# Two hybrid decoder layers on one core: the eight expert passes alternate between the 128-row and the 64-row form

## The reference, cut to what matters

```
def swiglu(h, w1, w3, w2):
    return (jax.nn.silu(h @ w1) * (h @ w3)) @ w2

def moe_swiglu(h, w_router, w1, w3, w2):
    logits = (h @ w_router).astype(jnp.float32)
    top_val, top_idx = lax.top_k(logits, TOP_K)          # TOP_K = 2
    top_w = jax.nn.softmax(top_val, axis=-1)
    combine = jnp.sum(jax.nn.one_hot(top_idx, N_EXPERTS) * top_w[..., None], axis=-2)
    out = jnp.zeros_like(h)
    for e in range(N_EXPERTS):                           # 8 experts, inner width 3584
        out = out + combine[..., e:e + 1] * swiglu(h, w1[e], w3[e], w2[e])
    return out
```

## Time and profile before

| | |
|---|---|
| median of three runs | 1884.23 us (1883.58 to 1884.46) |
| profiled execution, its own time | 1884.23 us |
| its span (first to last instruction) | 1882.5 us |
| PE busy | 1807.6 us, 96% |
| DVE busy | 1527.5 us, 81% |
| ACT busy | 1240.2 us, 66% |
| read from memory | 511.74 MB |

### The profile page before, as it was taken

How to read it: one execution, slowest core, us unless ns; L and a number is a source line. 1 busy time by engine, 2 the same in 40 slices (tenths; PEclk the granted TensorE clock), 3 DMA queues, 4 the chain that set the end, 5 groups by cost and what they waited for, 6 DMA issues and landing times.

```text
span 1882.5 us, 25226 instructions
## 1 busy us (share of the span) xinstructions
PE 1807.6 (96%) x10094; PEld 1534.7 (82%) x10094; DVE 1527.5 (81%) x1402; ACT 1240.2 (66%) x1144; POOL 73.8 (4%) x97
## 2 busy tenths in 40 slices
PE   9999999999999999999999999999998989888897
PEld 9989998999999998998878888888886656666665
DVE  7999965575568999764688888888889979889796
ACT  5656745454455565655667777777778878788785
POOL 1000000100010000000100000001000000000000
PEclk9999999999999999999999999999999999999998
DMA  8544544355545445553689999999999999999992
GB/s 331 179 176 154 183 162 183 140 188 180 197 166 181 179 138 196 204 182 132 226 319 402 377 379 362 406 370 364 401 363 390 421 350 419 382 372 416 353 418 109
DMA packets 75845, 519.91 MB, mean 276 GB/s; under 512 B 9360, under 2 KB 9616, under 8 KB 14544
## 3 DMA queue, kind: packets, MB, share of 16 engines
q1 hardware_dynamic: 72464, 507.84, 70.3%
q0 software_dynamic: 2544, 9.18, 1.7%
q10 hardware_dynamic: 720, 1.31, 0.2%
HBM read 511.74 MB, written 6.55 MB: 275 GB/s over the span
## 4 chain that ended last, share of the span: by engine, by line
PE 77%; DVE 10%; ACT 6%; issue 5%; DMA 1%; SPq 0%; ACTq 0%; DVEq 0%
PE psum L1903 15%; PE psum L1889 13%; PE psum L1891 13%; PE psum L1890 13%; PE psum L1904 7%; DVE wlo L1164 7%; ACT whi L629 5%; PE psum L2391 5%; PE psum L2392 4%; PE psum L2410 1%; PE psum L2404 1%; DVE U L1742 1%; PE psum L2157 1%; PE psum L2137 1%; DMA raw<-in_stream 1%
## 5 line engine op out<-in xcount | busy, mean ns | idle before, releaser
L1164 DVE TENSOR_TENSOR wlo<-raw,whi 128x2048 fp32r<-128x2048 f32 x369 | 839.0, 2281 | 214.9 <-ACT whi L629 214.3
L629 ACT ACTIVATE whi<-raw 128x2048 fp32r<-128x2048 f32 x369 | 699.3, 1902 | 150.3 <-PE psum L1891 76.9
L1903 PE MATMUL psum<-h_hl,whi 128*128 128x512 f32 x1216 | 430.3, 398 | 0.3 <-DVE U L1522 0.2
L1904 PE MATMUL psum<-h_hl,wlo 128*128 128x256 f32 x1216 | 340.1, 280 | 0.0
L2391 PE MATMUL psum<-whi,act_hl 128*128 128x512 f32 x672 | 286.6, 426 | 41.0 <-DVE wlo L1164 36.9
L1889 PE MATMUL psum<-whi,act_hl 128*128 128x512 f32 x736 | 291.3, 396 | 4.3 <-DVE wlo L1164 4.1
L1891 PE MATMUL psum<-whi,act_hl 128*128 128x512 f32 x736 | 287.5, 391 | 0.0
L1890 PE MATMUL psum<-wlo,act_hl 128*128 128x512 f32 x736 | 287.2, 390 | 0.0
L1903 PEld LDWEIGHTS psum<-h_hl,whi 128*128 128x128 f32 x1216 | 228.2, 188 | 55.3 <-issue 1.2
L2392 PE MATMUL psum<-wlo,act_hl 128*128 128x512 f32 x672 | 269.2, 401 | 0.0
L1904 PEld LDWEIGHTS psum<-h_hl,wlo 128*128 128x128 f32 x1216 | 229.5, 189 | 0.1
(11 more groups left out here) (291 smaller groups left out, 2076.3 us busy)
## 6 DMA issues: line engine op xcount, KB each, us to landing
raw<-in_stream SPq DMA_DIRECT2D x366, 1024.0 KB, 6.7
U<-in_stream SPq DMA_DIRECT2D x74, 1024.0 KB, 7.4
memhat<-in_stream SPq DMA_DIRECT2D x37, 1024.0 KB, 7.3
raw<-in_stream SPq DMA_DIRECT2D x6, 512.0 KB, 3.7
xacc<-U POOLq DMA_DIRECT2D x3, 512.0 KB, 7.6
xT<-in_x_cols ACTq DMA_DIRECT2D x4, 256.0 KB, 6.5
raw<-in_stream SPq DMA_DIRECT2D x4, 256.0 KB, 6.9
memhat<-in_mem_cols SPq DMA_DIRECT2D x1, 1024.0 KB, 20.0
```

The costliest lines, as they stand in the source:

```text
L629: act.activation(whi[:, n % SPLIT, 0:words], src[:, 0:words], ACT.Copy).then_inc(hi_ready, 1)
L1164: dve.tensor_tensor(wlo[:, n % SPLIT, 0:words], src[:, 0:words], whi[:, n % SPLIT, 0:words].bitcast(F32), ALU.subtract).then_inc(lo_ready, 1)
L1903: pe.matmul(o[:].rearrange("p (a b) -> p a b", a=2), st[0], mv, start=start, stop=False)
L1904: return pe.matmul(o[:, 0:256], st[1], mv[:, 0, :], start=False, stop=stop)
```

## The change

`few(p)` is true for the odd passes and no longer for p of 4 and above, so the order of forms is full, few, full, few, and so on. The tables follow: the ranks 1 to 4 go to passes 1, 3, 5, 7 and the ranks above to passes 2, 4, 6; `cap` and the slots of the experts likewise. `folded_rows` leaves the branch that only a few step has, because now a full pass comes after a few pass and has to fold its result.

```
 def few(p):
-    return p >= NE // 2
+    return p % 2 == 1

 def folds(p, f):
-    return (FSTEPS + 1) * (p - NE // 2) + f
+    return (FSTEPS + 1) * (p // 2) + f
...
-            gp.iota(rank_at[:, NE // 2:NE], pattern=[[1, NE // 2]], base=1, channel_multiplier=0,
+            gp.iota(rank_at[:, 1:NE:2], pattern=[[1, NE // 2]], base=1, channel_multiplier=0,
...
-            gp.iota(rank_at[:, 0:NE // 2], pattern=[[1, NE // 2]], base=NE // 2, channel_multiplier=0,
+            gp.iota(rank_at[:, 0:NE:2], pattern=[[1, NE // 2]], base=NE // 2, channel_multiplier=0,
...
-            gp.memset(cap[:, 0:NE // 2], float(SLOTS)).then_inc(rt_const, 1)
+            gp.memset(cap[:, 0:NE:2], float(SLOTS)).then_inc(rt_const, 1)
...
-                                in_slots(slice(1, NE // 2), iota, posp, b)
-                                ins = in_slots(slice(NE // 2, NE), iota_few, posp, b)
+                                in_slots(slice(1, NE, 2), iota_few, posp, b)
+                                ins = in_slots(slice(2, NE, 2), iota, posp, b)
...
-                            if f == 0 and p and few(p - 1):
-                                folded_rows(p - 1)
                             if few(p):
                                 folded_gate(p, f)
+                        if f == 0 and p and few(p - 1):
+                            folded_rows(p - 1)
```

## The result

The changed kernel takes 1895.55 us, the median of four runs (1893.9 to 1896.32), against 1883.9 us for four runs of the kernel before (1882.31 to 1884.46): a ratio of 1.0062 with a 95% interval of 1.0044 to 1.0080, so 8 to 15 us slower. Timed again beside the experiments it took 1892.18 us (1890.89 to 1895.58, 6 runs) against 1884.5 (1880.27 to 1888.45, 29 runs), a ratio of 1.0044 (1.0030 to 1.0058). The forecast was 1891 in a range of 1885.5 to 1895.5: the direction and the mechanism held, the first measurement lies just above the range.

The account below looks back on a forecast made before the run. PE was taken to bound full passes, the loop of splits and PE the few passes. Hand-overs 13.9, less 10.0 given back, plus 3.2 for the clock made +7.1 on 1884.2: 1891 us, range 1885.5 to 1895.5.

Parts of the forecast that it names:

- What bounds the passes: Full passes go at PE's pace, few passes at the loop of ACT's split, DVE's split and PE; weights arrive in time.
- rival D: The weight stream sets the few passes' pace, so hand-over losses are waited for anyway: no change, 1884 us; chance 0.07.
- The full pass behind a few pass: Folding 1.72 us plus PE's 2.9 us stop before c5: 4.6 us extra, 123.5 us a pass, 13.9 us for three.
- Given back, 3 x 3.34 = 10.0: A few pass is 3.34 us cheaper behind a full pass than behind a few pass; three such save 10.0 us.
- B: At few-to-full hand-overs ACT and DVE hide the wait, leaving only 1.72 us of folding: faster, 1879.3 us; chance 0.08.
- C: c1 or c2 of the full pass also waits, 1 to 2 us more per hand-over: 1894 to 1897 us; chance 0.10.
- The clock: PE's clock falls to 0.50 behind the new stops in full passes, 1.6 us each; none to three, 0 to 4.8 us.
- I take two, 3.2: Two of the three new stops before c5 in full passes are followed by a clock fall, 3.2 us in all.
- The falls at the few passes' ends: Clock falls at the few passes' ends stay four in both orders, counted 0, shifting up to 1.5 us either way.

Follow-up runs that it names:

- three moves: Kernel before with ScalarE's copy moved to c7, VectorE's last-step product ahead of c40 and remainder of transposed rows ahead of c41: 1859.86 us, ratio 0.9864.
- with the stop filled: Changed kernel with ten unread matmuls in PE's stop ahead of c5: 1888.0 us; with 13 more at each few pass's end: 1880.88 us.
- both edits: Changed kernel with ScalarE's copy of folded rows moved from c5 to c7: 1879.17 us; or with PE's fold moved from behind c3 to behind c1: 1879.99 us.
- alternating kernel: The changed kernel (full, few, full, few) against the kernel before: 1895.55 us, ratio 1.0062; timed again 1892.18 us, ratio 1.0044.
- block order: The order of the kernel before, four full then four few passes: 1883.9 us; 1884.5 us beside the experiments.
- block_early_product: Kernel before with VectorE's product of a few pass's last step moved from behind the split of c40 to ahead of it: 1879.22 us, ratio 0.9973.
- the versions with the early product: VectorE's last-step product ahead of c40's split: kernel before 1879.22 us, with late copy 1871.17, with a third move 1859.86; changed kernel with late copy 1874.31.
- one_swap: Changed kernel with few passes 1, 5, 6 and 7 in place of 1, 3, 5 and 7: 1888.44 us, ratio 1.0015 against the kernel before.

## Why the prediction was right in its mechanism, and which step failed

**What bounds the passes: right.** Full passes at PE's pace, few passes at the pace of the splits, the stream not waited for. The few pass with three moves at 410 GB/s shows that there was room in the stream; rival D is out. (The prediction read the clock as full but for the last slice; a 9 stands for 90% or more, and the trace before has falls of 3.4 us at 911.6 and 945.7 in pass 0.)

**The full pass behind a few pass, 4.6 us over 118.85: right.** 123.39 to 123.45 us in six passes with the stop filled, against 123.5 worked out. The stop was 2.71 us in the trace where 2.75 was expected, the fold 1.6 where 1.7 was.

**Given back, 3 x 3.34 = 10.0: right in size.** 9.8 us in the two profiles (6.7 and 3.1). The prediction did not divide the 3.34: 0.6 is the clock's.

**Rivals B and C.** The wait wasn't hidden, and the splits' order is why: both edits that leave the work as it is and move the wait bring the full pass to 120.4. C didn't occur; PE waited for no chunk between c0 and c5.

**The clock: this step failed.** The size of one fall, 1.6 us in a full pass, was right; how many there would be was not. "I don't take all three for certain ... I take two, 3.2" was a term that was mis-sized: all three falls came, in both profiles of the alternating kernel, 4.8 us. With that the sum is 13.9 - 10.0 + 4.8 = 8.7, or 1892.9, which agrees with the second measurement (ratio 1.0044, 8 us). And "The falls at the few passes' ends ... I take 0", with 1.5 us in all either way, was too narrow: such a fall costs 1.5 us or, where it lasts twice as long, 2.5, at each of four ends. The falls in pass 0 stood in no term at all, though the clock was at 0.50 there for 6.8 us in the profile before, 10.2 in the first of the alternating kernel and never in the second; between these two pass 1 moved by 4.8 us. The first measurement's 11.65 us are 3 more than the corrected sum. (One of the rows leaned on shows less than was read from it: the stretch 1409 to 1413 of the earlier trace rows ends where the stop of 1.66 us ends; the trace has 1.00 behind it too, from 1413 to 1417.)

**The range was too narrow for the measurement.** The three runs shown before agreed within 0.9 us, and I read this as the spread of the kernel. Over 29 executions the same kernel went from 1880.27 to 1888.45, and the mean granted clock of each execution goes with it: 0.987 in the two slowest (1888.4 us), 0.988 in six from 1886.4 to 1887.3, 0.990 in ten from 1882.8 to 1885.1, 0.991 in eight from 1880.3 to 1884.4. So most of the spread is how much of an execution PE spent at 0.50. The first measurement fits: its four executions have 0.987, 0.987, 0.988 and 0.989 (1895.81, 1896.32, 1895.28, 1893.9 us), those of the second 0.988 to 0.990. The step from 1892.9 to 1895.55 is thus, as far as these means tell, falls at places that the sum left at nothing. Which places they were in the executions that were not profiled stays open, and so does a remainder of some 4 us between executions of the same mean. That the first lay outside the range and the second inside is chance.

## What to carry to other kernels

Work out the price of a hand-over between two regimes for each ordered pair of regimes, and ask at each which in-order engine has a wait on the slow one's result ahead of work that the next regime needs at once; alternation multiplies those hand-overs. A small instruction that waits costs not its own time but the head start of everything queued behind it: moving the copy by two splits was worth 13 us in the alternating order and 8 in the block order, and three such moves 25 in the block order. When a stop is removed, look for the next small instruction behind a long one on the same engine before the gain is counted.

## What the runs showed of the hardware that I had not expected

- TensorE's granted clock went to 0.50 at or within 1.1 us behind each stop of 2.71 us in the two profiles of the alternating kernel and each of 2.77 us in the kernel before (1.2 GHz instead of 2.4); ten unread matmuls in the stop kept it at 1.00. The length of a stop alone doesn't decide it: in block_early_product one of three such stops (2.77 us, ending at 1651.63) was followed by 1.00, of nine stops of 2.26 to 2.40 us in the versions with the early product four had a fall, and in one_swap 0.50 began 1.2 us behind a stop of 1.83 us (ending at 1544.20), where such stops of 1.6 to 1.8 us had none in the other profiles; the stop of 1.9 us in pass 0 (ending at 942.90 in the first profile of the alternating kernel) had one there and none in the second.
- Executions of one program on one core differed by 8 us (1880.27 to 1888.45), with a mean granted clock of 0.991 in the fastest and 0.987 in the slowest.
- The same fall costs 1.6 us where PE is the bound and 0.6 where the splits are, so that a stop of nearly the same length is dearer in the busier pass.
- Behind the same stop of 3.56 us the clock was at 0.50 for 3.4 us in one execution and 6.8 in another, of the same program; the pass took 112.9 and 113.9 us.
